# The short convolution of the second layer reads its input in PSUM instead of an SBUF copy

## The reference, cut to what matters

```python
def causal_depthwise_conv(x, w, b):          # CONV_WIDTH_2 = 4
    S = x.shape[1]
    xp = jnp.pad(x, ((0, 0), (CONV_WIDTH_2 - 1, 0), (0, 0)))
    out = b
    for k in range(CONV_WIDTH_2):
        out = out + xp[:, k:k + S] * w[k]
    return out

def rg_lru(x, w_a, b_a, w_x, b_x, lam):      # blocks of 64 channels
    r = jax.nn.sigmoid(einsum('bsgi,gij->bsgj', xb, w_a) + b_a)
    i = jax.nn.sigmoid(einsum('bsgi,gij->bsgj', xb, w_x) + b_x)
    log_a = -LRU_C * r * jax.nn.softplus(-lam)
    a = jnp.exp(log_a)
    b_in = jnp.sqrt(-jnp.expm1(2.0 * log_a)) * (i * x)
    # h_t = a_t * h_(t-1) + b_in_t, as an associative scan

# in hybrid_layer: z = rms_norm(x) @ w_in, cut into q, c_kv, ..., g_attn, x_rnn, g_rnn, merge
h = rg_lru(causal_depthwise_conv(x_rnn, conv_w, conv_b), ...)
y_rnn = (h * jax.nn.silu(g_rnn)) @ w_rnn_proj
mixed = sigmoid(merge_a) * y_attn + sigmoid(merge_r) * y_rnn
```

## Time and profile before

| | |
|---|---|
| median of 3 runs | 2138.19 us (2137.8 to 2143.58) |
| the profiled execution | 2140.61 us |
| its span (first to last instruction) | 2138.8 us |
| mean granted TensorE clock | 0.993 |
| PE busy | 2072.8 us, 97% |
| DVE busy | 1449.0 us, 68% |
| ACT busy | 1008.9 us, 47% |
| POOL busy | 1019.5 us, 48% |
| matmuls | 11809 |

### The profile page before, as it was taken

One profiled execution on the slowest core, in us unless ns is written; L12 is line 12 of the kernel. 1 busy time (PEld: TensorE's weight loads), 2 busy tenths in 40 slices (PEclk: granted clock), 3 DMA queues, 4 the chain that ended last, 5 costly groups with the idle time before them and its releaser, 6 DMA issues.

```text
span 2138.8 us, 31665 instructions
## 1 busy us (share of the span) xinstructions
PE 2072.8 (97%) x11809; PEld 1857.5 (87%) x11809; DVE 1449.0 (68%) x2805; ACT 1008.9 (47%) x1843; POOL 1019.5 (48%) x571
## 2 busy tenths in 40 slices
PE   8998999999999999999999999999999989999998
PEld 7745789999999999999999999999867777876677
DVE  4235548859997667878778888877688844017853
ACT  4237433368888743333333333334456542336632
POOL 3210355655456666665666666563425544430032
PEclk9999999999999999999999999999999999999999
DMA  5230224557768899999899999994212223220021
GB/s 196 78 96 11 64 84 154 164 194 262 259 237 316 317 337 340 333 345 363 314 346 344 341 333 356 333 339 167 101 60 89 79 80 107 91 77 1 1 79 60
DMA packets 145623, 419.67 MB, mean 196 GB/s; under 512 B 13504, under 2 KB 60224, under 8 KB 143680
## 3 DMA queue, kind: packets, MB, share of 16 engines
q1 hardware_dynamic: 108608, 283.42, 38.7%
q0 software_dynamic: 36864, 134.23, 16.8%
HBM read 375.06 MB, written 42.53 MB: 195 GB/s over the span
## 4 chain that ended last, share of the span: by engine, by line
PE 91%; ACT 3%; DVE 3%; issue 2%; DMA 1%; SPq 0%; POOL 0%; DVEq 0%; ACTq 0%
PE bank L473 24%; PE bank L474 24%; PE bank L475 24%; PE bank L853 4%; PE bank L1032 2%; PE bank L640 1%; PE bank L1051 1%; PE wide L1051 1%; PE bank L734 1%; PE bank L735 1%; PE bank L736 1%; PE wide L493 1%; DMA wraw<-in_wstream 1%; PE wide L1041 1%; PE wide L598 1%
## 5 line engine op out<-in xcount | busy, mean ns | idle before, releaser
L2505 POOL TENSOR_TENSOR wl<-wraw,wh 128x1024 fp32r<-128x1024 f32 x273 | 687.6, 2522 | 707.3 <-ACT wh L1168 707.1
L473 PE MATMUL bank<-XH,wh 128*128 128x384 f32 (+2 forms) x1616 | 573.1, 355 | 13.8 <-issue 10.3
L474 PE MATMUL bank<-XL,wh 128*128 128x384 f32 (+2 forms) x1616 | 565.9, 350 | 0.0
L475 PE MATMUL bank<-XH,wl 128*128 128x384 f32 (+2 forms) x1616 | 562.9, 348 | 0.0
L1168 ACT CAST wh<-wraw 128x1024 fp32r<-128x1024 f32 x362 | 378.6, 1046 | 194.2 <-PE bank L475 164.1
L473 PE MATMUL bank<-WTH,wh 128*128 128x384 f32 x1024 | 343.3, 335 | 1.0 <-issue 0.8
L475 PE MATMUL bank<-WTH,wl 128*128 128x384 f32 x1024 | 342.8, 335 | 0.0
L474 PE MATMUL bank<-WTL,wh 128*128 128x384 f32 x1024 | 342.5, 334 | 0.0
L473 PEld LDWEIGHTS bank<-XH,wh 128*128 128x128 f32 x1616 | 304.8, 189 | 42.6 <-issue 20.5
L474 PEld LDWEIGHTS bank<-XL,wh 128*128 128x128 f32 x1616 | 305.0, 189 | 21.0 <-issue 2.1
L475 PEld LDWEIGHTS bank<-XH,wl 128*128 128x128 f32 x1616 | 305.8, 189 | 19.3
(11 more groups left out here) (517 smaller groups left out, 3240.9 us busy)
## 6 DMA issues: line engine op xcount, KB each, us to landing
wraw<-in_wstream SPq DMA_DIRECT2D x362, 512.0 KB, 4.4
g_scratch<-gs SPq DMA_DIRECT2D x12, 2048.0 KB, 7.4
gr<-g_scratch SPq DMA_DIRECT2D x15, 1536.0 KB, 13.4
a_scratch<-tmp SPq DMA_DIRECT2D x72, 192.0 KB, 1.9
tmp<-a_scratch SPq DMA_DIRECT2D x46, 192.0 KB, 7.0
sq<-a_scratch SPq DMA_DIRECT2D x26, 192.0 KB, 8.9
shifted<-hc_scratch SPq DMA_DIRECT2D x12, 270.0 KB, 4.8
h<-in_hT SPq DMA_DIRECT2D x8, 264.0 KB, 6.5
```

The source lines that it names most:

```text
L473: pe.matmul(o, w1, x1, start=n == 0, stop=False)
L474: pe.matmul(o, w1, x2, start=False, stop=False)
L475: m = pe.matmul(o, w2, x1, start=False, stop=n == len(ks) - 1)
L2505: return pool.tensor_tensor(lo, src, hi.bitcast(F32), ALU.subtract)
```

## The change

The copy on ACT goes, and with it the signal `branch_x` and the two memsets of the zero columns on POOL. DVE's four taps read the bank of xr(c) itself. The order of the taps is turned round: the first, over all 512 columns, is now the one with the newest token (weight 3), and the tap that reaches k tokens back adds to columns k to 511 only, from columns 0 to 511-k of the bank. DVE waits for the product instead of the copy. The bank's freed event, which PE waits for before it takes the bank again, was the copy (`branch_x`) and is now the last tap (`branch_conv` 3).

```diff
-        product(XH, XL, *full(("xr", 0), (branch_x, 0)), x_ready=second_ready)
+        product(XH, XL, *full(("xr", 0), (branch_conv, (0, 3))), x_ready=second_ready)
         next(latent_steps)
         for c in range(8):
             if c + 1 < 8:
-                product(XH, XL, *full(("xr", c + 1), (branch_x, c + 1)))
+                product(XH, XL, *full(("xr", c + 1), (branch_conv, (c + 1, 3))))
             branch_gates(c)
...
-        def branch_in(c):
-            act.wait_ge(*gemm.at("xr", c))
-            if c > 1:
-                act.wait_ge(*branch_conv.at(c - 2, 3))
-            act.copy(xrs[c % 2][:, 3:515], bank_of["xr", c][:, :]).then_inc(*branch_x.tell(c))
-
         stream()
-        branch_in(0)
...
             if c < 7:
-                branch_in(c + 1)
                 stream()
...
         def branch_in(c):
-            xr, xc = xrs[c % 2], xcs[c % 2][:, 0:512]
-            dve.wait_ge(*branch_x.at(c))
-            dve.wait_ge(*pad_done.at("xr", c % 2))
+            xr, xc = bank_of["xr", c], xcs[c % 2][:, 0:512]
+            dve.wait_ge(*gemm.at("xr", c))
             if c > 1:
                 dve.wait_ge(*branch_step.at(c - 2, "yx"))
-            dve.tensor_scalar(xc, xr[:, 0:512], g("conv_w2", c * 4), g("conv_b2", c), ALU.mult,
+            dve.tensor_scalar(xc, xr[:, :], g("conv_w2", c * 4 + 3), g("conv_b2", c), ALU.mult,
                               ALU.add).then_inc(*branch_conv.tell((c, 0)))
             for k in range(1, 4):
                 dve.wait_ge(*branch_conv.at(c, k - 1))
-                dve.scalar_tensor_tensor(xc, xr[:, k:k + 512], g("conv_w2", c * 4 + k), xc, ALU.mult,
-                                         ALU.add).then_inc(*branch_conv.tell((c, k)))
+                dve.scalar_tensor_tensor(xc[:, k:512], xr[:, 0:512 - k], g("conv_w2", c * 4 + 3 - k), xc[:, k:512],
+                                         ALU.mult, ALU.add).then_inc(*branch_conv.tell((c, k)))
...
-        pool.wait_ge(*idx_mm.at(7, 3))
-        for i in range(2):
-            pool.memset(xrs[i][:, 0:3], 0.0).then_inc(*pad_done.tell(("xr", i)))
         stream()
```

More of the change, by code:

```diff
@@ L379, in build_program @@
     relued, summed, topped = signal("relued"), signal("summed"), signal("topped")
-    branch_x, branch_conv, branch_mm = signal("branch_x"), signal("branch_conv"), signal("branch_mm")
+    branch_conv, branch_mm = signal("branch_conv"), signal("branch_mm")
     branch_sig, branch_act, branch_step = signal("branch_sig"), signal("branch_act"), signal("branch_step")
```

## The result

| | before | changed |
|---|---|---|
| median of 4 runs each | 2140.89 us | 2156.7 us |
| range of the runs | 2137.8 to 2144.12 | 2156.12 to 2157.86 |
| profiled execution, span | 2138.8 us | 2153.9 us |
| mean granted clock | 0.993 | 0.990 |

Ratio 1.0062, 95% interval 1.0045 to 1.0078; the median of the kernel before moved from 2138.19 to 2140.89 as runs were added. The same kernel timed a second time, in 6 runs against 11, had 1.0081 (1.0066 to 1.0097). So the change costs 13 to 17 us by the ratios, 15.8 by the medians both times: slower, as forecast, but by more than the 9.3 us, and outside the range (2144 to 2153). Of the 9.2 us between 2156.7 and the forecast 2147.5, 2.7 are the moved median of the kernel before.

What follows compares the result with a forecast made beforehand. PE, busy 97% of the span, was taken to bound the kernel. Later mg products summed to 2.6 + 1.5 + 5.7 - 0.2 - 0.3 = +9.3 us, a forecast median of 2147.5 us, range 2144 to 2153.

Steps and rivals of the forecast that it cites:

- What bounds the kernel: Whole kernel: PE is busy 97% of the span, so other engines' changes matter only through PE's pauses.
- the copy's price: ACT in the branch: removing eight copies of 0.58 us gains nothing, since ACT idles 4.2 us in every round.
- The bank as the new last wait: Ahead of mg(0) to mg(5), PE waits for the fourth tap to free the bank: +2.6, +1.5 and +5.7 us.
- The two small terms: End of the branch: mg(6) starts earlier, -0.2 us, and chunk 6's tanh is freed from blocked taps, -0.3 us.
- At mg(0): First mg product: it waits for chunk 1's taps, whose start is left at 1588.18, and comes 2.6 us later.
- The taps' freedom from POOL: DVE's taps in the rounds: reading PSUM, they are not held up by POOL; DVE gains 5.3 us a round.
- rival A: First tap in the rounds: still held up by POOL, in all +14.8 us, 2153 us; chance 0.09.
- The term C: Four taps of a chunk from PSUM: 0.68, three of 0.685 and gaps of 0.04, in sum 2.86 us.
- Rival B: PE's clock falls in the new pauses, 1.3 us each, six times +7.8, in all +17, 2155 us; chance 0.05.
- Rival C: Not slower: taps done before POOL's low part of mg(c)'s weights, so the bank costs nothing; 2137.7 us; chance 0.05.

Runs made afterwards that it cites:

- own_banks: Changed kernel, taps reading PSUM without a copy, but xr(c) made in two banks of its own outside the ring of four; ratio 0.9999 to the kernel before.
- taps_first: Changed kernel with DVE's taps of chunk c+2 ahead of the top-k round and those of chunk 1 ahead of lambda's small steps; ratio 0.9997 to the kernel before.
- hold: Kernel before, copy and SBUF taps kept, but the bank of xr(c) counts as free only after the fourth tap; ratio 1.0239 to the kernel before.
- imm_taps: Changed kernel with constants 0.5 and 0.01 in the taps instead of per-partition weights and bias; ratio 1.005 to the kernel before.
- pool_ahead: Kernel before, with POOL's low part of mg(c+1)'s weights made ahead of its wait for chunk c's gated result; ratio 0.9959 to the kernel before.

## Why the prediction was wrong in size

**What bounds the kernel, and the copy's price: right.** own_banks removes the same copies and memsets and is as fast as the kernel before.

**The bank as the new last wait: right, in each of its places.** The named pauses appeared ahead of mg(0) to mg(5) and not at mg(6). In the rounds the taps' place in DVE's queue, behind the top-k round, was the reason: taps_first takes it away and with it the loss. hold shows the event alone. The two small terms came out too: without the clock mg(6) came 0.2 earlier after mg(5), and the last stretch, mg(6) to the last mg product, is 24.50 us instead of 24.79 (forecast: -0.3). At mg(0) 3.05 us were lost and not 2.6: 0.3 by the taps of chunk 1, and 0.16 because they started later: the taps of chunk 0, ahead of them in DVE's queue, are 0.27 us longer too, and the prediction had left that start as it was.

**The taps' freedom from POOL: right.** The first tap, for which I had no row, isn't held up (0.80 us beside POOL's `wl`); rival A is out. By the Trainium skill ("SBUF — State Buffer", "SBUF: two separate sides") DVE needs the ports that it shares with POOL only for two SBUF inputs or a two-port mode. The trace agrees: 24 of 24 taps within 747 to 752 ns, many of them beside POOL. The Trainium skill's advice to copy first where many operations follow ("VectorE: DVE Perf Modes", "Rules for kernel authors") makes no difference either way off the path: own_banks, without the copy, has 0.9999.

**The term C = 2.86 us: mis-sized, 3.16 measured.** I took 0.685 us from L2248 and 0.68 for the first tap. L2248's scalar is the constant 0.125 in the instruction; the taps' are columns of `gn`. The trace of before had the difference: the SBUF tap with such a scalar takes 0.75, and I put its longer time down to SBUF. imm_taps gave 0.689 and 0.680. Six places of 0.30: 1.8 us. This is the first step that failed.

**Rival B, priced at all or nothing: partly true.** The second step that failed, and the larger one, is the clock: my sum has no term for it. I weighed the new pauses of 2.2 to 2.6 us by the nearer of two rows (2.19, clock kept) and gave 0.05 to a fall. They became 2.5 us (2.9 ahead of mg(0)), and the clock fell behind two of six, 1.6 us each, 3.2 us in all. My range had no case with a few falls. The price of 1.3 us was too low too: it counted 3 us behind the pause of 5.48 us, and the slow stretch there goes on to about 1734.3, so it costs some 2.1 us (an estimate: half of the 4.3 us from 1729.97).

The sum with both: 9.3 + 1.8 + 3.2 = 14.3, against 14.4 measured in the branch. With the 0.16 us at mg(0) it is 14.5. The remainder to the medians' 15.8, and between the two ratios, is within what the runs scatter.

**Rival C, not slower: wrong, and its point of decision right.** The taps ended behind the low part, so the bank cost its time. Where they end ahead of it (taps_first), or the bank is out of the ring (own_banks), the time is that of the kernel before; of the chain through copy and taps only 0.33 us came back in own_banks, where I had 0.5, and not 7.

## What to carry to other kernels

Whoever lets a reader use a PSUM bank instead of a copy moves the bank's release from the copy to the reader's last instruction, and with it to everything that stands in the reader's queue ahead of it. So look up who takes the bank next, and put the reader's work ahead of what nobody waits for, or give the product a bank outside the ring; only if DVE is on the path does the saved work pay. And price an instruction by a row of the same operands, scalars too.

## What the runs showed of the hardware

- A per-partition scalar operand of a DVE instruction that reads some 512 fp32 columns from PSUM costs 0.06 us: 0.748 against 0.689, and with two of them 0.802 against 0.680.
- TensorE's clock fell to the lower level (1.2 GHz) behind two of the changed kernel's six pauses of 2.5 to 2.9 us, the same ones in two profiles and not the longest; behind one of six of 2.17 to 2.27 us (imm_taps); and in hold behind all seven, one of 2.47 us and six of 7.0 to 7.4. A fall behind a pause of 2.2 to 2.5 us cost 1.6 us, in hold 1.3 to 2.8. With the pauses cut to 0.77 us (1.17 ahead of mg(0)) by matmuls without a use it never fell in these places.
- It also falls without a pause: in the kernel before, PE runs 32 matmuls of one column each from 1513.10 to 1517.40 with no idle time, and the clock is at 0.50 from 1516 to 1522.
- A pause shown as 0.77 us costs 1.00 us of distance (19.42 against 18.42 us for the round, kernel before and pool_ahead).
- A DVE instruction with one operand in PSUM is not held up by POOL's work in SBUF (24 of 24 taps within 747 to 752 ns); those with all operands in SBUF can be (four taps 8.2 us instead of 2.9, "ix" 1.29 instead of 0.68).
